# An output projection over 512 columns a product, with the samples' halves packed into one load

## What is computed

```
def merge_branches(x, o_a, o_b, o_m, za, zb, zm, gates, w_proj_a, w_proj_b, w_proj_m, w_out):
    ...
    g = jax.nn.sigmoid(gates).reshape(b, t, N_BRANCH, D_MODEL)
    mixed = g[:, :, 0] * p_a + g[:, :, 1] * p_b + g[:, :, 2] * p_m
    return x + mixed @ w_out
...
y_prompt = rms_norm(h_p, g_final)
y_sample = rms_norm(h_s, g_final)
```

## Time and profile before

| | |
|---|---|
| timed runs, median (lowest to highest) | 661.34 us (660.77 to 661.66) |
| the profiled execution's own time | 659.01 us |
| its span, first to last instruction | 657.3 us |
| TensorE busy | 618.4 us, 94% |
| ScalarE, VectorE busy | 277.1 us (42%), 320.7 us (49%) |
| mean granted clock of TensorE | 0.995 |

### The profile page before, as it was taken

The page is one execution under the profiler, slowest core; times in us unless marked ns, Lnnn a source line. Parts: engine busy times, 40 slices in busy tenths (PEclk is TensorE's granted clock), DMA queues, the critical chain, the costliest instruction groups (busy, mean ns, idle before and its releaser), DMA issues.

```text
span 657.3 us, 12343 instructions
## 1 busy us (share of the span) xinstructions
PE 618.4 (94%) x5074; PEld 570.1 (87%) x5074; DVE 320.7 (49%) x673; ACT 277.1 (42%) x548; POOL 98.0 (15%) x182
## 2 busy tenths in 40 slices
PE   2899999999899999999999998798999999999996
PEld 1899999887689999999888874498999999999986
DVE  3942112766433857557474545548227145244334
ACT  4944333565454333346555445545232322321222
POOL 3010100000002315667223221201000000000000
PEclk9999999999999999999999998999999999999998
DMA  8663732222045756775421534206323232232103
GB/s 271 223 210 104 262 133 66 65 65 65 1 131 186 211 162 197 235 240 171 144 90 42 175 103 155 96 2 227 129 65 104 90 115 78 88 106 65 33 3 129
DMA packets 58776, 82.74 MB, mean 126 GB/s; under 512 B 4608, under 2 KB 48192, under 8 KB 58464
## 3 DMA queue, kind: packets, MB, share of 16 engines
q1 hardware_dynamic: 49808, 55.58, 25.9%
q0 software_dynamic: 8912, 26.37, 13.2%
HBM read 74.69 MB, written 7.24 MB: 125 GB/s over the span
## 4 chain that ended last, share of the span: by engine, by line
PE 83%; DMA 6%; DVE 4%; ACT 3%; issue 2%; POOL 1%; SPq 0%; POOLq 0%; DVEq 0%; ACTq 0%
PE pj L691 18%; PE pj L692 17%; PE pj L693 17%; DMA out<-stage 3%; PE pj L1025 3%; PE pj L1027 3%; PE pj L1026 3%; PE pt_bank L797 2%; PE po_bank L834 2%; PE ps L691 2%; PE ps L692 2%; PE ps L693 2%; DMA w_raw<-in_w_mem_kv 2%; DVE w_lo L1351 1%; PE ps L751 1%
## 5 line engine op out<-in xcount | busy, mean ns | idle before, releaser
L691 PE MATMUL pj<-xh,w_hi 128*128 128x260 f32 x1024 | 293.5, 287 | 0.0
L692 PE MATMUL pj<-xh,w_lo 128*128 128x260 f32 x1024 | 289.1, 282 | 0.0
L693 PE MATMUL pj<-xl,w_hi 128*128 128x260 f32 x1024 | 288.9, 282 | 0.0
L691 PEld LDWEIGHTS pj<-xh,w_hi 128*128 128x128 f32 x1024 | 192.8, 188 | 7.7 <-issue 5.6
L692 PEld LDWEIGHTS pj<-xh,w_lo 128*128 128x128 f32 x1024 | 192.8, 188 | 0.0
L693 PEld LDWEIGHTS pj<-xl,w_hi 128*128 128x128 f32 x1024 | 192.8, 188 | 0.0
L1351 DVE TENSOR_TENSOR w_lo<-w_raw,w_hi 128x1024 fp32r<-128x1024 f32 x84 | 99.5, 1220 | 176.3 <-ACT w_hi L1052 176.2
L1052 ACT ACTIVATE w_hi<-w_raw 128x1024 fp32r<-128x1024 f32 x84 | 84.5, 1049 | 24.9 <-PE pj L1027 22.7
L1109 ACT ACTIVATE gate<-pj 128x260 f32<-128x260 f32 x48 | 18.5, 386 | 82.6 <-PE pj L693 82.6
L1109 ACT ACTIVATE region<-pj 128x260 f32<-128x260 f32 x44 | 17.0, 386 | 73.1 <-PE pj L693 73.0
L1025 PE MATMUL pj<-w_hi,mixh 128*128 128x256 f32 (+1 forms) x160 | 45.0, 281 | 1.2 <-DVE w_lo L1351 0.8
(11 more groups left out here) (264 smaller groups left out, 892.9 us busy)
## 6 DMA issues: line engine op xcount, KB each, us to landing
w_raw<-in_w_in SPq DMA_DIRECT2D x64, 512.0 KB, 4.3
ring<-in_cache_diff_kv POOLq DMA_DIRECT2D x32, 256.0 KB, 3.5
out<-stage SPq DMA_DIRECT2D x19, 256.0 KB
ring<-in_cache_mem_kv POOLq DMA_DIRECT2D x16, 256.0 KB, 3.8
w_raw<-in_w_out SPq DMA_DIRECT2D x8, 512.0 KB, 4.0
w_raw<-in_w_mem_kv SPq DMA_DIRECT2D x4, 512.0 KB, 10.9
region<-in_x_prompt SPq DMA_DIRECT2D x4, 512.0 KB, 11.3
q_all<-q_rows POOLq DMA_DIRECT2D x8, 256.0 KB, 3.8
```

The costliest lines, as they stand in the source:

```text
L691: pe.matmul(out, wh, mh, start=(i == 0), stop=False)
L692: pe.matmul(out, wl, mh, start=False, stop=False)
L693: last = pe.matmul(out, wh, ml, start=False, stop=(i == n - 1))
```

## The change

It does four things. The first two output chunks move forward in the list, behind (in, 21) and (in, 22), and get memory of their own, 512 columns side by side (`wide_hi` in the memory of `oz`, `wide_lo` in that which `y_nat` had); the other two go into the two slots as before, and a product takes both. So the projection has two column halves c and ten units, in four banks in turn. For the sample tile, ScalarE packs the high half of its mixture into columns 0 to 7 and the low half into columns 32 to 39 of one stationary operand of 40 columns (`mixs`), which is multiplied with the weights' high and low parts, 16 products; the crossing rows 32 to 39 are copied out and added. The residual rows lie where the split input was (`xh`, `xl`) and load after the last projection is evacuated. The sum of squares is taken in two halves, and the first is turned into a bias of the root.

```
@@ -53,8 +53,9 @@
     beside_bm = [("in", 20), ("in", 24)]
     third = [("in", 28), ("proj", 0)]
     for m in range(1, 4):
-        third += [("in", 20 + m), ("in", 24 + m), ("in", 28 + m), ("proj", m)]
-    return first, beside_a, second, beside_bm, third, [("out", m) for m in range(4)]
+        early_out = [("out", m - 1)] if m < 3 else []
+        third += [("in", 20 + m)] + early_out + [("in", 24 + m), ("in", 28 + m), ("proj", m)]
+    return first, beside_a, second, beside_bm, third, [("out", 2), ("out", 3)]
...
     SEQ = sum(PARTS, [])
     N_A, N_SECOND, N_BM, N_THIRD, N_OUT = (sum(map(len, PARTS[:i])) for i in range(1, 6))
     POS = {k: n for n, k in enumerate(SEQ)}
+    IN_SLOTS = [n for n, k in enumerate(SEQ) if k not in (("out", 0), ("out", 1))]
+    W_SLOT = {n: i % 2 for i, n in enumerate(IN_SLOTS)}
+
+    def two_on(n):
+
+        later = IN_SLOTS[IN_SLOTS.index(n) + 1:][:2]
+        return range(later[0] + 1, later[1] + 1) if len(later) == 2 else ()
...
+        y_nat = sb("y_nat", [128, 5, D], f32, early)
+        early.close()
         xh = sb("xh", [128, KT, TT], f32r)
         xl = sb("xl", [128, KT, TT], f32r)
         w_raw = sb("w_raw", [128, 3, 4, CW])
         w_hi = sb("w_hi", [128, 2, KT, CW], f32r)
         w_lo = sb("w_lo", [128, 2, KT, CW], f32r)
+        wide_hi = sb("wide_hi", [128, KT, 512], f32r, early)
+        early.close()
         oz = sb("oz", [128, KT, TT])
...
         mix_t = sb("mix_t", [128, 2, 3, HALF], f32, early)
-        y_nat = sb("y_nat", [128, 5, D], f32, early)
+        wide_lo = sb("wide_lo", [128, KT, 512], f32r, early)
+        mixs = sb("mixs", [128, KT, 40], f32r, early)
         early.close()
+        y_cross = gate[0:NS, 2, :, :].rearrange("p a b -> p (a b)")
...
-        OUT_ORDER = [(m, t) for m in range(2) for t in range(5)] + [(m, t) for t in OUT_TILES for m in (2, 3)]
+        OUT_ORDER = [(0, t) for t in range(5)] + [(1, t) for t in OUT_TILES]
+        out_banks = [pj[0][:, :], pj[1][:, :], bank[0], bank[3]]
@@ -632,10 +651,12 @@
             pool.wait_ge(s_so, 2)
             for i in range(2):
                 pool.wait_ge(s_out[i], OUTC[i])
+            pool.memset(mixs[:, :, :].bitcast(f32), 0.0).then_inc(s_mz, 1)
+            pool.dma_start(g_fin[:, :], ins["g_final"].unsqueeze(0).partition_broadcast(128).rearrange("p a d -> p (a d)")).then_inc(s_gf, 16)
+            pool.wait_ge(s_ev, U0[-1])
             for t in range(4):
                 pool.dma_start(y_nat[:, t, :], x_p[128 * t:128 * t + 128, :]).then_inc(s_yl, 16)
             pool.dma_start(y_nat[0:NS, 4, :], x_s).then_inc(s_yl, 16)
-            pool.dma_start(g_fin[:, :], ins["g_final"].unsqueeze(0).partition_broadcast(128).rearrange("p a d -> p (a d)")).then_inc(s_gf, 16)
...
-            for i, (m, t) in enumerate(OUT_ORDER):
-                n = N_OUT + m
-                pe.wait_ge(s_lo, 2 * n + 2)
-                rows = rows_of(t)
-                if i >= 2:
-                    pe.wait_ge(s_y, i - 1)
-                out = pj[i % 2][0:rows, 0:CW]
+            for i, (c, t) in enumerate(OUT_ORDER):
+                pe.wait_ge(s_lo, 2 * POS["out", 2 * c + 1] + 2)
+                if i in (2, 3):
+                    pe.wait_ge(s_mx, 13 + i)
+                if i >= 4:
+                    pe.wait_ge(s_y, i - 3)
+                if t == 4:
+                    pe.wait_ge(s_ms, 2)
+                out = out_banks[i % 4][0:(40 if t == 4 else 128), :]
                 for kt in range(KT):
-                    if m == 0 and t < 3:
+                    if c == 0:
+                        wh, wl = wide_hi[:, kt, :], wide_lo[:, kt, :]
+                    else:
+                        wh, wl = w_hi[:, :, kt, :], w_lo[:, :, kt, :]
+                        out = out_banks[i % 4][0:(40 if t == 4 else 128), :].rearrange("p (a b) -> p a b", a=2)
+                    if t == 4:
+                        ms = mixs[:, kt, :]
+                        pe.matmul(out, ms, wh, start=(kt == 0), stop=False)
+                        last = pe.matmul(out, ms, wl, start=False, stop=(kt == KT - 1))
+                        continue
+                    if c == 0 and t < 3:
                         pe.wait_ge(s_ml, 2 * kt + (1 if t < 2 else 2))
-                    mh = mixh[:, kt, 128 * t:128 * t + rows]
-                    ml = mixl[:, kt, 128 * t:128 * t + rows]
-                    pe.matmul(out, mh, w_hi[:, n % 2, kt, :], start=(kt == 0), stop=False)
-                    pe.matmul(out, ml, w_hi[:, n % 2, kt, :], start=False, stop=False)
-                    last = pe.matmul(out, mh, w_lo[:, n % 2, kt, :], start=False, stop=(kt == KT - 1))
+                    mh = mixh[:, kt, 128 * t:128 * t + 128]
+                    ml = mixl[:, kt, 128 * t:128 * t + 128]
+                    pe.matmul(out, mh, wh, start=(kt == 0), stop=False)
+                    pe.matmul(out, ml, wh, start=False, stop=False)
+                    last = pe.matmul(out, mh, wl, start=False, stop=(kt == KT - 1))
                 last.then_inc(s_po, 1)
...
+        def high_half(n, s):
+            if n in W_SLOT:
+                return w_hi[:, W_SLOT[n], 4 * s:4 * s + 4, :]
+            return wide_hi[:, 4 * s:4 * s + 4, CW * SEQ[n][1]:CW * SEQ[n][1] + CW]
...
             def hi_split(n, halves=(0, 1)):
 
-                if n >= len(SEQ):
-                    return
-                if n >= 2:
-                    wait_chunk_used(act, n - 2)
+                if n not in W_SLOT:
+                    act.wait_ge(s_ol, 3)
+                elif n >= 2:
+                    wait_chunk_used(act, IN_SLOTS[IN_SLOTS.index(n) - 2])
                 for s in halves:
                     m = 2 * n + s
                     act.wait_ge(s_raw[m % 3], RAW_AT[m])
-                    act.activation(w_hi[:, n % 2, 4 * s:4 * s + 4, :], w_raw[:, m % 3, :, :], ACT.Copy).then_inc(s_hi, 1)
+                    act.activation(high_half(n, s), w_raw[:, m % 3, :, :], ACT.Copy).then_inc(s_hi, 1)
...
@@ -1310,25 +1351,36 @@
                 for g in range(3 if m else 0):
                     n = POS["in", 20 + 4 * g + m]
                     evacuate(n)
-                    hi_split(n + 2)
+                    for later in two_on(n):
+                        hi_split(later)
                 for i in range(4 * m, 4 * m + 4):
                     c, hf = divmod(i, 2)
                     act.wait_ge(s_mix, i + 1)
                     act.activation(mixh[:, c, HALF * hf:HALF * hf + HALF], mix_t[:, i % 2, 0, :], ACT.Copy).then_inc(s_mh, 1)
-                hi_split(POS["proj", m] + 2)
-            for m in range(4):
-                hi_split(N_OUT + m + 2)
-            for j, t in enumerate(OUT_TILES):
+                if m == 3:
+                    act.wait_ge(s_ml, 16)
+                    act.wait_ge(s_mz, 1)
+                    act.activation(mixs[:, :, 0:NS], mixh[:, :, T:TT], ACT.Copy).then_inc(s_ms, 1)
+                    act.activation(mixs[:, :, 32:32 + NS], mixl[:, :, T:TT], ACT.Copy).then_inc(s_ms, 1)
+                for later in two_on(POS["proj", m]):
+                    hi_split(later)
+            for i, (c, t) in enumerate(OUT_ORDER):
                 r = rows_of(t)
...
+                cols = slice(512 * c, 512 * c + 512)
+                if t == 4:
+                    act.wait_ge(s_po, i + 1)
+                    act.activation(y_cross[:, cols], out_banks[i % 4][32:32 + NS, :], ACT.Copy).then_inc(s_yx, 1)
+                act.wait_ge(s_y, i + 1)
+                if i:
+                    act.wait_ge(s_ysq, i)
+                part = ssq[0:r, 8 * c + t:8 * c + t + 1]
+                act.activation(gate[0:r, 0, :, 0:256], y_nat[0:r, t, cols].rearrange("p (a c) -> p a c", c=256),
+                               ACT.Square, accum_out=part).then_inc(s_ysq, 1)
+                if c:
+                    act.wait_ge(s_ysq, i + 1)
+                    act.wait_ge(s_yb, t + 1)
+                    act.activation(rstd[0:r, 8 + t:9 + t], part, ACT.Sqrt, scale=1.0 / D,
+                                   bias=rstd[0:r, t:t + 1]).then_inc(s_ystd, 1)
...
@@ -1695,7 +1745,8 @@
 
             for m in range(4):
                 for g in range(3 if m else 0):
-                    lo_split(POS["in", 20 + 4 * g + m] + 2)
+                    for later in two_on(POS["in", 20 + 4 * g + m]):
+                        lo_split(later)
...
                 mixed_lo(4 * m + 3)
-                lo_split(POS["proj", m] + 2)
+                for later in two_on(POS["proj", m]):
+                    lo_split(later)
...
+            def first_variance(t):
+                r = rows_of(t)
+                dve.wait_ge(s_ysq, t + 1)
+                dve.tensor_scalar(rstd[0:r, t:t + 1], ssq[0:r, t:t + 1], 1.0 / D, EPS, ALU.mult,
+                                  ALU.add).then_inc(s_yb, 1)
+
+            for i, (c, t) in enumerate(OUT_ORDER):
                 r = rows_of(t)
                 dve.wait_ge(s_po, i + 1)
-                y = y_nat[0:r, t, CW * m:CW * m + CW]
```

(54 more changed lines are left out.)

12 lines of the change are left out of this document (removed).

## The result

The changed kernel took **670.42 us** (median; 667.09 to 671.55) against 661.06 us for the kernel before, run beside it: a ratio of 1.012 (95% interval 1.009 to 1.015). A second series on the chip gave 667.39 against 660.18, 1.011 (1.008 to 1.014). The forecast was 664.5 with a range up to 668.0. The direction and the mechanism came as forecast; two sizes did not: the pace of a 512-column product and the price of the clock.

What follows compares the result with a forecast made beforehand. TensorE, busy 94% of the span, was taken to bound the kernel. Terms -8.1 + 8.6 + 2.4 + 0.3 = +3.2 us gave 664.5 us on a timed median of 661.34, range 660.4 to 668.0.

Steps and rivals of the forecast that it cites:

- Part 1: Output projection: 480 products of 256 columns become 224 of 512, at 225.0 ns full and 220.9 packed; gain 8.1 us.
- Part 3: Behind both third-stage waits: the clock falls to half rate, 1.2 us lost each, 2.4 us in all; bounds 0 and 3.4.
- 2.0 us of waits: Output projection before the change: the part of its 58.4 us beyond the units' 56.4, expected to go.
- 388 against 282 ns: Trace durations of f32r products with 512 and 256 columns, 106 ns apart, cited as agreeing with 106.7 ns for 256 more columns.
- Rival (d): Output stage: wide products cost in proportion, 236.7 ns, gain 5.4 us, sum +5.9, 667.2 us; chance 0.06.
- the forecast's own sign, over 52 us: An output stage under 49 or over 52 us would show the forecast wrong; about 50 us would show it right.
- Part 2: Third stage, two output chunks split early: TensorE waits 4.3 us behind m = 0 and m = 1, 8.6 us lost.
- rival (a): Third stage: the waits come but the clock stays at 2.4 GHz, sum +0.8 us, 662.1 us; chance 0.18.
- Part 4: End of the kernel: the last addition covers 512 columns instead of 256, 0.3 us lost; bounds 0 and 0.4.
- Part 5: Residual rows loading behind the last evacuation, samples' packing, crossing copies and variance in halves: put at nothing.
- Rival (c): Third stage: no wait, so the gain stands alone, sum -7.8 us, 653.5 us; chance 0.12.

Runs made afterwards that it cites:

- paces: The changed kernel with its out-chunk splits moved between evacuations, plus six series of 48 unread products behind the output stage: 120.2 ns at 256 columns, 234.0 at 512.
- warm: The changed kernel with 32 unread 128x260 products more on TensorE at each of its two third-stage waits: 663.39 us, ratio 1.004 to the kernel before.
- reorder: The changed kernel with output chunks 0 and 1 behind (in, 24+m) in the list, their halves split between ScalarE's evacuations: 654.64 us, ratio 0.993 to the kernel before.
- residual: The kernel before with only the residual rows moved into the input's memory and loaded after the last gate unit is evacuated: 661.39 us, ratio 1.000.

## Why the forecast was wrong, step by step

Two terms failed, both by size: the pace taken for a 512-column product (Part 1, 225.0 ns forecast, 231.3 measured) and the price of the clock behind the waits (Part 3, 2.4 us forecast, 3.1 to 3.8 measured). The waits themselves came as forecast.

**Part 1 (forecast -8.1, measured -6.3): the first mis-sized term.** The pace did not hold: "118.3 ns plus 256 more columns at 2.4 GHz" takes the 11.7 ns above the columns as the same at any width. Measured they grow, to 18.0 at 512 columns (231.3 - 213.3). And the 4.1 ns taken off for a narrow stationary operand are not there: packed products follow at 3.69 us for 16, 230.6 ns. At 256 columns they are: 114.2 against 118.3 ns with 8, 117.7 against 120.2 with 40 (paces); at 512 columns they are not. With the measured paces 192 x 231.3 + 32 x 230.6 = 51.8 us, and 52.1 is what the stage takes. Of the 1.8 us missed 1.2 are the full products, 0.3 the packed ones, and 0.2 the time from the last product to its addition: the "2.0 us of waits" that were to go held 1.8 us of waits and this, which stays. The row that misled was 388 against 282 ns. It is not the one product of 512 columns in the trace, as the forecast has it: it is 64 rows deep, not 128, and the other two of its line last longer:

```profile
L757 PE MATMUL ps<-k0h,q0h 64*128 64x512 f32 x16 | 4.9, 600 | 0.0
...
L757 PE MATMUL ps<-k0l,q0h 64*128 64x512 f32 x16 | 3.3, 396 | 0.0
```

388, 396 and 600 ns for one shape: that one of the three differs from 282 by 106 ns agreed with the assumption by chance, where the paces turned out to be 113 apart. Rival (d) was a little nearer, 53.0 us against 52.1 where the forecast had 50.3, and should have had more weight: the forecast's own sign, over 52 us, is met by a little. The formula in the Trainium skill's page "TensorE: Matmul & The Clock Gate", section "Back-to-back issue gap", which that section gives for an isolated product, makes about 215.8 ns of 512 columns, 15 ns less than is measured here.

**Part 2 (forecast +8.6): right.** Two waits of 4.0 and 4.1 us by the rows, 4.3 and 4.4 from start to start, and 8.9 us for both by what the third stage of warm keeps. ScalarE waits for the transfer 2.96 and 3.09 us where "some 3 us" were forecast, and the cause is the one named, an order in which the fourth half needs the buffer of the first: reorder changes that order alone, in the list and on ScalarE, and the loss goes. Not all of a wait is the transfer: without those 2.96 us, by the rows above, TensorE would still have waited an estimated 1.2 us for the two copies more that stand ahead of the evacuation. Reorder takes both away at once; no run here parts them.

**Part 3 (forecast +2.4, measured 3.1 to 3.8 by the third stage of warm, 3.2 and 4.4 by the stretches of the two profiles): the second mis-sized term.** The clock falls behind both waits in both profiles of the changed kernel, and rival (a) falls with that. But the forecast took the middle between a fall 2.3 us into the wait and one at its end. In the first profile's second wait the fall comes at the end, which was the bad bound, 1.7 us; in its first wait it comes earlier, but 5.4 us are worked at half rate behind it, longer than the 3.4 us of the one row of before that showed it. The bound of 3.4 for both was taken from that one place, and it was too low for the first profile. In the second profile both lie near the bad bound, 1.7 and 1.5 us.

**Part 4 (+0.3): right.** The stretch behind the last addition went from 6.0 to 6.2 us.

**Part 5 (nothing): right.** VectorE never waited for the residual rows: its first addition comes straight behind its last split of weights, as the timeline of the second profile of the changed kernel shows,

```profile
611.77 2.36 DVE L1401 TENSOR_TENSOR w_lo<-w_raw,w_hi 128x1024 fp32r<-128x1024 f32 x2 [1.48 <-ACT w_hi L1093]
614.05 0.68 DVE L1801 TENSOR_TENSOR y_nat<-pj,y_nat 128x512 f32<-128x512 f32 x1
```

and that split, which ends a little after the first unit, holds up nobody, with three more banks to fill. The residual rows' move alone costs nothing measurable (residual).

**The sum** with the measured sizes is -6.3 + 8.9 + 3.5 + 0.2 = +6.3: on the 661.06 of the first series 667.4, which is inside the range, and on the 660.18 of the second 666.5 where 667.39 was measured. That the first series gave 670.42 is another 3 us, and these go with the clock as well: the mean granted clock of its four executions is 0.986 to 0.991, that of the six of the second series 0.989 to 0.993. A mean clock of c over a span S loses at most (1 - c) x S; with each execution's own loss taken off, the medians of the two series are the same, 661.4 us. In the first profile the longer stretch behind the first wait is 1 us of it, and the fall near 412, ahead of the third stage, an estimated 1.7 (3.4 us at half rate). Why the clock fell more often in that series stays open, and no run shows that the change has a part in the fall near 412; a profile of the kernel before has one at 404. Rival (c), no wait, fell for this kernel; the reorder is that case, 5.5 us below before where (c) had 7.8, and Part 1's 1.8 us are most of the difference. That the range held the second series and not the first is the clock's doing, and no merit of the sum.

## What to carry to other kernels

Look at where moved work stands, and not only at whether its engine has time for it: here the same splits cost 12 us in front of four evacuations that TensorE, the bounding engine, waits for, and nothing between them. Count a shared ring of buffers in the new order: the transfer that came late here was the one whose slot the moved work had just taken. Take the price of a product from the pace of a series of its shape and not from the duration of one: of one line and shape they lasted 388, 396 and 600 ns here. And take the price of a wait from wait and clock together: here 4.3 us of waiting became some 6 (5.9 to 6.5 by the third stage).

## What was not expected of the hardware

- The pace of fp32r products, each with a load of 128 stationary columns of its own, grows by 0.44 ns a column between 256 and 512 columns (120.2, 176.5, 234.0 ns), and at 128 columns it is still 110.4 ns, twice its columns' 53.3. What sets that floor was not tried.
- 40 or 8 stationary columns in place of 128 do not make a series of 512-column products faster by more than 2 ns a product; at 256 columns they save 2.5 to 4.1 ns. So the samples' tile costs by the number of its products, and packing saves by dropping one in three.
- One wait of 4 us cost 1.5 to 2.7 us more at 1.2 GHz (two places, two profiles), and the same place differed by 1 us between two executions of one kernel.
